# Seven Strassen products for the first four weight blocks of the up projection in eight of eleven steps

## The chip, the core and the metric

One NeuronCore of a Trainium2 chip runs the whole program. The metric is the device time of one execution in microseconds (us), here the median of three runs. Four engines work beside each other, each in the order of its own instruction list, and they hand work over by semaphores: TensorE (PE, with its weight loads PEld), VectorE (DVE), ScalarE (ACT) and GpSimd (POOL). SyncE (SP) issues nearly all DMA transfers.

## The reference, cut to what matters

One transformer block on 256 tokens of width 2048. The change touches the channel mixer's first product alone, `h @ w_up[l]`, which is 256 x 2048 times 2048 x 11264:

```python
h = rmsnorm(x, g_ffn_pre[l])
u = causal_dwconv(h @ w_up[l], ffn_conv_w[l])
gate, val = jnp.split(u, 2, axis=-1)
x = x + rmsnorm((jax.nn.silu(gate) * val) @ w_down[l], g_ffn_post[l])
```

## The kernel before, in words

All weights are float32 and come from device memory once. A block is 256 x 512 weights (512 KB, two slices of 128 rows, `KB = 2`); it lands in one of four buffers `raw` (`RING = 4`). TensorE works on halves of each number: ScalarE rounds a block to `w_hi` (`split` of ScalarE, L608), VectorE subtracts to get `w_lo` (`split` of VectorE, L989), and TensorE adds three matmuls for each pair of operands (activations hi by weights hi, hi by lo, lo by hi; L1486 to L1488). With two slices and two tiles of 128 tokens (`NT = 2`) a block is 12 matmuls of 128 x 512.

The up projection has 11 steps (`NUP`). A step makes 512 gate columns and the 512 value columns that belong to them: 8 blocks into `ACC[0]` (gate, half 0), then 8 into `ACC[1]` (value, half 1), 192 matmuls. Three counters pace the ring. `hi_ready` and `lo_ready` count the blocks that ScalarE and VectorE have split, `block_done` those that TensorE has used. ScalarE may overwrite slot i when `block_done` has reached the block four before; SyncE may load into `raw` slot i once `lo_ready` says that VectorE has read it.

Between the splits the same engines treat the results of the step before, at fixed places in their lists (`gate_done`, `value_done`): ScalarE copies each finished half out of PSUM (`up_evacuate`, L897), SyncE moves its 32 x 32 squares with 16 small transfers (`move_squares`, L482, four after each of four loads), VectorE transposes the squares (`up_turn`, L1316), ScalarE does the first tap of the depthwise convolution (`up_first_tap`, L907), VectorE the other two (`up_tap`, L1323, four instructions each), ScalarE the Silu of the gate (L921), VectorE the product with the value half (L1352), ScalarE rounds it (`act_hi`, L931) and VectorE subtracts (`act_lo`, L1355). Step 0 is written out; steps 1 to 10 are a loop on every engine.

## Time and profile before

| | |
|---|---|
| time, median of 3 runs | 1642.23 us (1642.19 to 1642.34) |
| the profiled execution | 1642.32 us, of which the span of the profile is 1640.5 us |
| PE busy | 1631.4 us (99%) |
| VectorE busy | 1012.3 us (62%) |
| ScalarE busy | 831.9 us (51%) |
| granted TensorE clock over the span | 0.998 |

A busy time is the union of an engine's instructions. Matmuls overlap their neighbours in the trace (0.39 us long, one begun every 0.23 us), so the pace of TensorE is read from what it releases, not from one instruction's length. A row's last bracket says how long the engine was idle before it and who ended that.

### The profile page before, as it was taken

To read this page: it belongs to the slowest core of one execution; us is meant where nothing else is said; L and a number is where in the kernel's file an instruction comes from. 1 tells how busy PE (TensorE), PEld (TensorE's weight loads), DVE (VectorE), ACT (ScalarE), POOL (GpSimd) and SP (SyncE) were. 2 spreads that over 40 slices of the span, in tenths; PEclk is the share of its full clock that TensorE was granted. 3 is DMA by queue.
4 is the path that set the end of the run, shared out by engine and by line. 5 is a ranking of instruction groups with operands and counts; after the bars stand their busy time and mean duration, and the time that the engine had idled before them with its cause. 6 is when DMAs were issued, how large, how long until landed. Compare 5 with 4: busy or idle time off the path is not lost.

```text
span 1640.5 us, 22316 instructions
## 1 busy us (share of the span) xinstructions
PE 1631.4 (99%) x7267; PEld 1346.6 (82%) x7267; DVE 1012.3 (62%) x1374; ACT 831.9 (51%) x1053; POOL 54.6 (3%) x117
## 2 busy tenths in 40 slices
...
GB/s 281 279 225 216 192 181 197 221 214 220 192 206 193 244 215 186 210 226 218 218 221 210 154 219 215 209 220 220 216 215 217 219 224 209 242 192 168 215 197 136
DMA packets 207784, 346.72 MB, mean 211 GB/s; under 512 B 28952, under 2 KB 52329, under 8 KB 207209
## 3 DMA queue, kind: packets, MB, share of 16 engines
...
q0 software_dynamic: 2048, 2.10, 0.4%
...
## 4 chain that ended last, share of the span: by engine, by line
PE 99%; DVE 0%; POOL 0%; DVEq 0%; issue 0%; ACT 0%; POOLq 0%; ACTq 0%
PE PS L1486 29%; PE PS L1488 28%; PE PS L1487 28%; PE PS L1620 3%; PE PS L1618 3%; PE PS L1619 3%; PE PS L1654 1%; PE PS L1656 1%; PE PS L1655 1%; PE PS L1567 0%; PE PS L1578 0%; PE PS L1507 0%; PE PS L1513 0%; PE PS L1501 0%; PE PS L1726 0%; PE PS L1724 0%
## 5 line engine op out<-in xcount | busy, mean ns | idle before, releaser
L989 DVE TENSOR_TENSOR w_lo<-raw,w_hi 128x1024 fp32r<-128x1024 f32 x567 | 690.5, 1224 | 569.4 <-ACT w_hi L608 568.3
L608 ACT ACTIVATE w_hi<-raw 128x1024 fp32r<-128x1024 f32 x567 | 597.5, 1059 | 629.1 <-PE PS L1488 558.7
L1486 PE MATMUL PS<-w_hi,hT_hi 128*128 128x512 f32 x1504 | 587.6, 391 | 0.0
L1488 PE MATMUL PS<-w_hi,hT_lo 128*128 128x512 f32 x1504 | 585.2, 389 | 0.0
L1487 PE MATMUL PS<-w_lo,hT_hi 128*128 128x512 f32 x1504 | 585.1, 389 | 0.0
L1486 PEld LDWEIGHTS PS<-w_hi,hT_hi 128*128 128x128 f32 x1504 | 282.3, 188 | 60.9 <-issue 2.7
L1488 PEld LDWEIGHTS PS<-w_hi,hT_lo 128*128 128x128 f32 x1504 | 282.3, 188 | 58.6
L1487 PEld LDWEIGHTS PS<-w_lo,hT_hi 128*128 128x128 f32 x1504 | 282.3, 188 | 58.5
L1486 PE MATMUL PS<-w_hi,act_hi 128*128 128x512 f32 x336 | 130.9, 390 | 0.0
L1488 PE MATMUL PS<-w_hi,act_lo 128*128 128x512 f32 x336 | 130.7, 389 | 0.0
L1487 PE MATMUL PS<-w_lo,act_hi 128*128 128x512 f32 x336 | 130.7, 389 | 0.0
L1486 PEld LDWEIGHTS PS<-w_hi,act_hi 128*128 128x128 f32 x336 | 63.1, 188 | 13.7 <-issue 0.4
L1487 PEld LDWEIGHTS PS<-w_lo,act_hi 128*128 128x128 f32 x336 | 63.1, 188 | 13.0
L1488 PEld LDWEIGHTS PS<-w_hi,act_lo 128*128 128x128 f32 x336 | 63.1, 188 | 13.0
L1486 PE MATMUL PS<-w_hi,memT_hi 128*128 128x512 f32 x124 | 48.7, 392 | 0.0
L1488 PE MATMUL PS<-w_hi,memT_lo 128*128 128x512 f32 x124 | 48.3, 390 | 0.0
L1487 PE MATMUL PS<-w_lo,memT_hi 128*128 128x512 f32 x124 | 48.2, 389 | 0.0
L897 ACT ACTIVATE up_stage<-PS,r_h 128x512 f32<-128x512 f32 x44 | 27.9, 687 | 36.7 <-PE PS L1488 36.4
L1486 PE MATMUL PS<-w_hi,mixT_hi 128*128 128x512 f32 x96 | 37.3, 389 | 0.0
L1487 PE MATMUL PS<-w_lo,mixT_hi 128*128 128x512 f32 x96 | 37.3, 389 | 0.0
L1488 PE MATMUL PS<-w_hi,mixT_lo 128*128 128x512 f32 x96 | 37.3, 389 | 0.0
L1323 DVE SCALAR_TENSOR_TENSOR value_conv<-turned_sb,up_taps,value_conv 128x255 f32 (+3 forms) x88 | 36.6, 481 | 0.0
...
## 6 DMA issues: line engine op xcount, KB each, us to landing
raw<-in_w_up_dram SPq DMA_DIRECT2D x176, 512.0 KB, 4.0
raw<-in_w_in_dram SPq DMA_DIRECT2D x112, 512.0 KB, 4.1
raw<-in_w_gate_dram SPq DMA_DIRECT2D x96, 512.0 KB, 4.5
raw<-in_w_down_dram SPq DMA_DIRECT2D x88, 512.0 KB, 4.1
raw<-in_w_mem_kv_dram SPq DMA_DIRECT2D x32, 512.0 KB, 5.8
raw<-in_w_o_dram SPq DMA_DIRECT2D x32, 512.0 KB, 4.2
...
raw<-in_w_conv_out_dram SPq DMA_DIRECT2D x16, 512.0 KB, 3.7
```

The lines of the kernel that those rows point to most:

```text
L608: nc.scalar.activation(w_hi[i % RING][:], raw[i % RING][:], ACT.Copy).then_inc(hi_ready, inc)
L897: last = nc.scalar.activation(up_stage[half][:, :, :, t, :], ACC[half][:, t, :].rearrange("p (b m n) -> p m b n", b=BPC, n=SQ), ACT.Copy, ...
L989: nc.vector.tensor_tensor(w_lo[i % RING][:], raw[i % RING][:], w_hi[i % RING][:].bitcast(F32), ALU.subtract).then_inc(lo_ready, inc)
L1323: last = nc.vector.scalar_tensor_tensor(out=d[:, 2 - m:TOK], in0=turned_ch[:, b, 0:TOK - 2 + m], scalar=up_taps[:, m, bass.ds(half * FK + ...
L1486: nc.tensor.matmul(o, a_hi, b_hi, start=first, stop=False)
L1487: nc.tensor.matmul(o, a_hi, b_lo, start=False, stop=False)
L1488: last = nc.tensor.matmul(o, a_lo, b_hi, start=False, stop=last_k)
L1618: nc.tensor.matmul(ACC[1][:, t, :], hi[:, k, s], w_hi[i % RING][:, c, :], start=k == 0, stop=False)
L1619: nc.tensor.matmul(ACC[1][:, t, :], hi[:, k, s], w_lo[i % RING][:, c, :], start=False, stop=False)
L1620: last = nc.tensor.matmul(ACC[1][:, t, :], lo[:, k, s], w_hi[i % RING][:, c, :], start=False, stop=k == HK - 1)
L1654: nc.tensor.matmul(acc[:, t, :], a_hi[:, k, s], b_hi, start=k == 0, stop=False)
L1655: nc.tensor.matmul(acc[:, t, :], a_hi[:, k, s], b_lo, start=False, stop=False)
```

## The change

In steps 1 to 8 the four blocks that cover the first 512 rows of the weights, for gate and value (B11 = rows 0 to 255 of the gate, B12 the same rows of the value, B21 and B22 rows 256 to 511), are multiplied with the four 128 x 256 pieces of the activations by the Winograd form of Strassen's scheme: seven products of 6 matmuls each in place of eight. Sums of activations are made once, in step 0 (`left_sums`). In each fast step VectorE makes four sums of weight blocks (`summed`, the first two in place in `raw`), and the splits of these seven operands take the ring slots. The shared partial results are passed on by ScalarE with four copies out of PSUM (`seed`), two into other PSUM banks, two, scaled, into SBUF (`u2_scaled`, `p5_scaled`). Because these two must be added to the value half, VectorE now copies the value half out (`value_evacuate`, eight instructions) in place of ScalarE. The last two blocks of a fast step are done tile by tile, so that the first value tile is ready 12 matmuls before the end. Steps 9 and 10 do what they did, but are written out.

```diff
+QUAD = 7
+FAST_END = 9
...
+    FASTS = FAST_END - 1
+    STD = 2 * CB - 4
+    FAST_UNITS = -(-(QUAD + STD) // RING) * RING
+    L_DN = N_UP + 2 * NUP * CB
+    N_DN = L_DN + FASTS * (FAST_UNITS - 2 * CB)
...
+u2_scaled = at("u2_scaled", RB + 36 * K, [P, CW])
+p5_scaled = at("p5_scaled", RB + 38 * K, [P, CW])
+S_hi = at("S_hi", RB + 40 * K, [P, 4, KB, P], F32R)
+h2_whole = at("h2_whole", RB + 80 * K, [P, 2 * KB, TOK])
+B_sum = at("B_sum", RB + 80 * K, [P, KB, CW])
+S_sum = at("S_sum", RB + 84 * K, [P, 4, KB, P])
+S_lo = at("S_lo", RB + 84 * K, [P, 4, KB, P], F32R)
...
+    def fast_load(j, m, free, kb, half):
+        sp.wait_ge(lo_ready, up_units(j) + free)
+        if not isinstance(j, int):
+            sp.sem_inc(stream_pace, 1)
+        sp.dma_start(raw[m % RING][:], cols(w_up, kb * KB, half * FF + j * CW)).then_inc(raw_in[m % RING], 16)
+    def fast_step(j, jp):
+        first = isinstance(j, int)
+        for m, (kb, half) in enumerate(((0, 0), (0, 1), (1, 1), (1, 0))):
+            fast_load(j, m, m - 3 if first else (-4, -3, -2, 0)[m], kb, half)
+            move_squares(jp, 0, m)
+        for m in range(4, 2 * CB):
+            half, kb = (0, m - 2) if m < CB + 2 else (1, m - CB)
+            fast_load(j, m, (3, 5, 6, 6)[m - 4] if m < 8 else m, kb, half)
+            if CB <= m < CB + P // SQ:
+                move_squares(jp, 1, m - CB)
     up_step(0, None)
-    up_step(1, 0)
-    with sp.Fori(2, NUP) as j:
+    fast_step(1, 0)
+    with sp.Fori(2, FAST_END) as j:
+        fast_step(j, j - 1)
+    for j in range(FAST_END, NUP):
         up_step(j, j - 1)
...
+        X, Y = ACC[0][:, 1, :], ACC[1][:, 0, :]
+        landed(0)
+        hi(0, raw[0], -3)
+        if not first:
+            landed(3)
+            hi(3, raw[3], -4)
+        summed(1)
+        hi(1, raw[0], -2)
+        if first:
+            up_evacuate(0, 1)
+            landed(3)
+            hi(3, raw[3], 0)
+        summed(3)
+        hi(2, B_sum, -1)
+        seed(ACC[0][:, 0, :], X, 1)
+        hi(0, raw[1], 1)
+        landed(2)
+        hi(1, raw[2], 2)
+        if not first:
+            act.wait_ge(up_out, 2 * jp + 2)
+        seed(u2_scaled[:], X, 3, scale=r_h2[:, 0:1])
+        seed(p5_scaled[:], Y, 2, scale=r_h2[:, 1:2])
+        summed(4)
+        hi(2, B_sum, 3)
+        act.wait_ge(up_out, 2 * jp + 2)
+        seed(ACC[1][:, 1, :], X, 5)
+        for s in range(STD):
+            u = QUAD + s
+            landed(4 + s)
+            hi(u % RING, raw[s % RING], u - RING + 1, 1 if s < STD - 1 else 1 + FAST_UNITS - QUAD - STD)
+            if s in (1, 4):
+                gate_done(jp, {1: 3, 4: 6}[s])
+            if s in (6, 10):
+                value_done(jp, {6: 3, 10: 7}[s])
+            if s == 8:
+                up_evacuate(j, 0)
...
+    def left_sums():
+        a11, a12, a21, a22 = (h2_whole[:, KB * k:KB * k + KB, t * P:(t + 1) * P] for t in range(NT) for k in range(2))
+        dve.wait_ge(block_done, N_UP + CB)
+        dve.wait_ge(mid_lo, len(MID))
+        nc.vector.tensor_tensor(h2_whole[:], h2_hi[:, 0:2 * KB, :].bitcast(F32), h2_lo[:, 0:2 * KB, :].bitcast(F32), ALU.add).then_inc(s_sums, 1)
+        dve.wait_ge(s_sums, 1)
+        nc.vector.tensor_tensor(S_sum[:, 0, :, :], a21, a22, ALU.add).then_inc(s_sums, 1)
+        nc.vector.tensor_tensor(S_sum[:, 2, :, :], a11, a21, ALU.subtract).then_inc(s_sums, 1)
+        dve.wait_ge(s_sums, 2)
+        nc.vector.tensor_tensor(S_sum[:, 1, :, :], S_sum[:, 0, :, :], a11, ALU.subtract).then_inc(s_sums, 1)
+        dve.wait_ge(s_sums, 4)
+        nc.vector.tensor_tensor(S_sum[:, 3, :, :], a12, S_sum[:, 1, :, :], ALU.subtract).then_inc(s_sums, 1)
+    def left_remainders():
+        dve.wait_ge(s_hi_done, 1)
+        nc.vector.tensor_tensor(S_lo[:], S_sum[:], S_hi[:].bitcast(F32), ALU.subtract).then_inc(s_ready, 1)
...
+    def value_evacuate(j, t):
+        if t == 0:
+            dve.wait_ge(value_first, j)
+            dve.wait_ge(up_in[1], 16 * (P // SQ) ** 2 * j)
+        else:
+            dve.wait_ge(block_done, up_units(j) + FAST_UNITS)
+        more = (u2_scaled, p5_scaled)[t]
+        for b in range(BPC):
+            w = slice(b * P, (b + 1) * P)
+            last = nc.vector.scalar_tensor_tensor(out=up_stage[1][:, :, b, t, :], in0=ACC[1][:, t, w].rearrange("p (m n) -> p m n", n=SQ),
+                                                  scalar=r_h2[:, t:t + 1], in1=more[:, w].rearrange("p (m n) -> p m n", n=SQ),
+                                                  op0=ALU.mult, op1=ALU.add)
+        last.then_inc((value_out, up_out)[t], 1)
...
+        def lo(count, slot, src, inc=1):
+            dve.wait_ge(hi_ready, n + count)
+            nc.vector.tensor_tensor(w_lo[slot][:], src[:], w_hi[slot][:].bitcast(F32), ALU.subtract).then_inc(lo_ready, inc)
+        def summed(dst, a, b):
+            nc.vector.tensor_tensor(dst[:], a[:], b[:], ALU.subtract).then_inc(b_sums, 1)
+        b11, b12, b22, b21 = raw
+        lo(1, 0, b11)
+        dve.wait_ge(raw_in[1], up_landed(j, 1))
+        summed(b11, b12, b11)
+        dve.wait_ge(raw_in[2], up_landed(j, 2))
+        summed(b12, b22, b12)
+        dve.wait_ge(b_sums, 4 * jp + 1)
+        summed(B_sum, b22, b11)
+        if not first:
+            lo(2, 3, b21)
+            value_evacuate(jp, 0)
+            lo(3, 1, b11)
+            value_evacuate(jp, 1)
+        else:
+            lo(2, 1, b11)
+            lo(3, 3, b21)
+        lo(4, 2, B_sum)
+        dve.wait_ge(b_sums, 4 * jp + 3)
+        summed(B_sum, b21, B_sum)
+        lo(5, 0, b12)
+        lo(6, 1, b22)
+        lo(7, 2, B_sum)
+        for s in range(STD):
+            u = QUAD + s
+            lo(u + 1, u % RING, raw[s % RING], 1 if s < STD - 1 else 1 + FAST_UNITS - QUAD - STD)
+            if s in (0, 2, 3):
+                gate_done(jp, {0: 2, 2: 4, 3: 5}[s])
+            if s in (5, 7, 8, 9, 11):
+                value_done(jp, {5: 2, 7: 4, 8: 5, 9: 6, 11: 7}[s])
...
+        def product(count, slot, hi, lo, o, start=False):
+            pe.wait_ge(lo_ready, n + count)
+            for c in range(KB):
+                nc.tensor.matmul(o, hi(c), w_hi[slot][:, c, :], start=start and c == 0, stop=False, skip_group_check=not start)
+                nc.tensor.matmul(o, hi(c), w_lo[slot][:, c, :], start=False, stop=False, skip_group_check=not start)
+                last = nc.tensor.matmul(o, lo(c), w_hi[slot][:, c, :], start=False, stop=c == KB - 1, skip_group_check=not start)
+            last.then_inc(block_done, 1)
+        def block(k, t):
+            return [lambda c, a=a: a[:, KB * k + c, t * P:(t + 1) * P] for a in (h2_hi, h2_lo)]
+        def left(m):
+            return [lambda c, a=a: a[:, m, c, :] for a in (S_hi, S_lo)]
+        pe.wait_ge(up_out, 2 * jp + 1)
+        product(1, 0, *block(0, 0), X, True)
+        pe.wait_ge(value_out, jp + 1)
+        product(2 if isinstance(j, int) else 3, 1, *left(0), Y, True)
+        pe.wait_ge(seeded, 4 * jp + 1)
+        product(4, 2, *left(1), X)
+        product(4, 3, *block(1, 0), ACC[0][:, 0, :])
+        pe.wait_ge(seeded, 4 * jp + 2)
+        product(5, 0, *left(2), X)
+        pe.wait_ge(seeded, 4 * jp + 3)
+        product(6, 1, *left(3), Y)
+        pe.wait_ge(seeded, 4 * jp + 4)
+        product(7, 2, *block(1, 1), X)
+        for u in range(QUAD, QUAD + CB - 2):
+            multiply(n, u, CB, h2_hi, h2_lo, lambda t: ACC[0][:, t, :], kb=2 + u - QUAD, onto=True)
+        for u in range(QUAD + CB - 2, QUAD + STD - 2):
+            multiply(n, u, CB, h2_hi, h2_lo, lambda t: ACC[1][:, t, :], kb=4 + u - QUAD - CB, onto=True)
+        for t in range(NT):
+            for u in range(QUAD + STD - 2, QUAD + STD):
+                if t == 0:
+                    pe.wait_ge(lo_ready, n + u + 1)
+                for c in range(KB):
+                    k, sl = DK + KB * (u - QUAD - STD) + c, slice(t * P, (t + 1) * P)
+                    b_hi, b_lo = w_hi[u % RING][:, c, :], w_lo[u % RING][:, c, :]
+                    nc.tensor.matmul(ACC[1][:, t, :], h2_hi[:, k, sl], b_hi, start=False, stop=False, skip_group_check=True)
+                    nc.tensor.matmul(ACC[1][:, t, :], h2_hi[:, k, sl], b_lo, start=False, stop=False, skip_group_check=True)
+                    last = nc.tensor.matmul(ACC[1][:, t, :], h2_lo[:, k, sl], b_hi, start=False, stop=k == DK - 1, skip_group_check=True)
...
```

VectorE, at the head of the loop over the steps. `w_lo_57` to `w_lo_60` are the four ring slots, `raw_49` to `raw_52` the four landing buffers. Before:

```order
L989 TENSOR_TENSOR w_lo_57<-raw_49,w_hi_53 128x1024 [waits hi_ready]
L988 REGISTER_ALU
L989 TENSOR_TENSOR w_lo_58<-raw_50,w_hi_54 128x1024 [waits hi_ready]
L988 REGISTER_ALU
L989 TENSOR_TENSOR w_lo_59<-raw_51,w_hi_55 128x1024 [waits hi_ready]
L1312 REGISTER_ALU
L1314 ISA [waits up_in_gate]
```

After (the row ahead of these is the split of `raw_49`, as before):

```order
L1589 TENSOR_TENSOR raw_49<-raw_50,raw_49 128x1024 [waits raw_in1]
L1589 TENSOR_TENSOR raw_50<-raw_51,raw_50 128x1024 [waits raw_in2]
L1597 ISA
L1589 TENSOR_TENSOR B_sum<-raw_51,raw_49 128x1024 [waits b_sums]
L1585 REGISTER_ALU
L1586 TENSOR_TENSOR w_lo_60<-raw_52,w_hi_56 128x1024 [waits hi_ready]
L1569 REGISTER_ALU [waits value_first]
L1575 SCALAR_TENSOR_TENSOR up_stage_168<-PS,r_h_76,u_scaled 128x4x32 [waits up_in_value]
L1575 SCALAR_TENSOR_TENSOR up_stage_168<-PS,r_h_76,u_scaled 128x4x32 x3
L1585 REGISTER_ALU
L1586 TENSOR_TENSOR w_lo_58<-raw_49,w_hi_54 128x1024 [waits hi_ready]
L1571 ISA
```

Three weight sums and the first half of the value copy now stand between the step's first split and its third.

ScalarE, at the same place. Before:

```order
L607 REGISTER_ALU [waits raw_in0]
L608 ACT_TABLE_LOAD
L608 ACTIVATE w_hi_53<-raw_49 128x1024 [waits block_done]
L607 REGISTER_ALU [waits raw_in1]
L608 ACTIVATE w_hi_54<-raw_50 128x1024 [waits block_done]
L607 REGISTER_ALU [waits raw_in2]
L608 ACTIVATE w_hi_55<-raw_51 128x1024 [waits block_done]
```

After:

```order
L1004 ISA [waits raw_in0]
L1005 ACTIVATE w_hi_53<-raw_49 128x1024 [waits block_done]
L1004 REGISTER_ALU [waits raw_in3]
L1005 ACTIVATE w_hi_56<-raw_52 128x1024 [waits block_done]
L1011 ISA
L1004 REGISTER_ALU [waits b_sums]
L1005 ACTIVATE w_hi_54<-raw_49 128x1024 [waits block_done]
L1011 REGISTER_ALU
L1004 REGISTER_ALU [waits b_sums]
L1005 ACTIVATE w_hi_55<-B_sum 128x1024 [waits block_done]
```

The second split is now that of `raw_52`, the fourth load, and the activation table is no longer loaded at the head of the loop.

ScalarE, at the Silu of the gate within the loop. Before:

```order
L607 REGISTER_ALU [waits raw_in2]
L608 ACTIVATE w_hi_55<-raw_51 128x1024 [waits block_done]
L921 ACT_TABLE_LOAD [waits up_conv]
L921 ACTIVATE gate_conv<-gate_conv 128x1024
L607 REGISTER_ALU [waits raw_in3]
```

After:

```order
L1004 REGISTER_ALU [waits raw_in0]
L1005 ACTIVATE w_hi_56<-raw_49 128x1024 [waits block_done]
L969 ACTIVATE gate_conv<-gate_conv 128x1024 [waits up_conv]
L1004 REGISTER_ALU [waits raw_in1]
L1005 ACTIVATE w_hi_53<-raw_50 128x1024 [waits block_done]
```

The table load ahead of the Silu is gone from the loop as well; one stands in step 1, ahead of it.

## Rows read from the trace of the kernel before

**Rows 1.** Page, part 1: span, and busy time of each engine

```profile
span 1640.5 us, 22316 instructions
...
PE 1631.4 (99%) x7267; PEld 1346.6 (82%) x7267; DVE 1012.3 (62%) x1374; ACT 831.9 (51%) x1053; POOL 54.6 (3%) x117
```

**Rows 2.** Page, part 4: shares of the chain that ended last, by engine

```profile
PE 99%; DVE 0%; POOL 0%; DVEq 0%; issue 0%; ACT 0%; POOLq 0%; ACTq 0%
```

**Rows 3.** Windows: one up step, and the time after the last matmul

```profile
core 0: us, PE busy (x) PEld busy (x) DVE busy (x) ACT busy (x) POOL busy (x), PEclk, DMA share, GB/s
...
980.03:1023.56 43.53, 43.53 (x194) 36.05 (x193) 30.34 (x43) 26.73 (x33) 0.00 (x0) 1.00 0.71 213
...
1632.90:1640.50 7.60, 0.03 (x1) 0.00 (x0) 3.50 (x6) 0.69 (x2) 0.73 (x2) 0.67 0.50 188
```

**Rows 4.** Waits from 900 to 1380 us: total us, times, longest us

```profile
DVE w_lo L989 <- ACT w_hi L608: 140.6, 97, 2.3
ACT w_hi L608 <- PE PS L1488: 116.5, 85, 1.7
```

**Rows 5.** Timeline of ACT: start us, length us, instruction, count, idle before and releaser

```profile
980.03 1.27 ACT L897 ACTIVATE up_stage<-PS,r_h 128x512 f32<-128x512 f32 x2 [1.74 <-PE PS L1488]
981.18 1.06 ACT L608 ACTIVATE w_hi<-raw 128x1024 fp32r<-128x1024 f32 x1
982.13 1.70 ACT L907 ACTIVATE value_conv<-turned_sb,up_taps 128x256 f32 x4
983.73 1.05 ACT L608 ACTIVATE w_hi<-raw 128x1024 fp32r<-128x1024 f32 x1
...
992.72 1.06 ACT L931 ACTIVATE act_hi<-value_conv  x1 [0.83 <-DVE value_conv L1352]
...
998.98 1.06 ACT L608 ACTIVATE w_hi<-raw 128x1024 fp32r<-128x1024 f32 x1 [1.65 <-PE PS L1488]
...
1012.20 1.28 ACT L921 ACT_TABLE_LOAD   x1 [1.28 <-DVE gate_conv L1323]
1013.50 1.06 ACT L921 ACTIVATE gate_conv<-gate_conv  x1
1014.46 1.99 ACT L608 ACTIVATE w_hi<-raw 128x1024 fp32r<-128x1024 f32 x2
```

**Rows 6.** Timeline of DVE in the same step

```profile
985.96 1.66 DVE L1323 SCALAR_TENSOR_TENSOR value_conv<-turned_sb,up_taps,value_conv 128x255 f32 x4
987.54 1.22 DVE L989 TENSOR_TENSOR w_lo<-raw,w_hi 128x1024 fp32r<-128x1024 f32 x1
...
991.39 1.21 DVE L1352 TENSOR_TENSOR value_conv<-gate_conv,value_conv  x1
...
1000.08 1.23 DVE L989 TENSOR_TENSOR w_lo<-raw,w_hi 128x1024 fp32r<-128x1024 f32 x1 [1.49 <-ACT w_hi L608]
1001.22 1.42 DVE L1316 STREAM_TRANSPOSE turned_sb<-up_moved 128x256 f32<-128x256 f32 x4
...
1010.44 1.66 DVE L1323 SCALAR_TENSOR_TENSOR gate_conv<-turned_sb,up_taps,gate_conv 128x254 f32 x4
```

**Rows 7.** Timeline of DVE at an evacuation of PSUM with two operands

```profile
190.09 2.15 DVE L1047 SCALAR_TENSOR_TENSOR proj_stage<-PS,r_x,cc_sb 128x128 f32<-128x128 f32 x8
192.25 0.69 DVE L1124 TENSOR_REDUCE top<-PS 128x2 f32<-128x512 f32 x1
```

**Rows 8.** Timeline of the SP queue, issues in the same step

```profile
989.80 0.39 SPq L325 DMA_DIRECT2D raw<-in_w_up_dram  x1
990.23 2.41 SPq L482 DMA_DIRECT2D up_moved<-up_stage  x4
992.97 0.38 SPq L325 DMA_DIRECT2D raw<-in_w_up_dram  x1
```

**Rows 9.** DMA issues of the up weights: count, KB each, median us to landing

```profile
raw<-in_w_up_dram SPq DMA_DIRECT2D x176, 512.0 KB, 4.0
```

**Rows 10.** Timeline of PE, its last matmul

```profile
1632.54 0.39 PE L1726 MATMUL PS<-w_hi,act_lo 128*128 128x512 f32 x1
```

More of the change, by code:

```diff
@@ L277, in build_block_kernel @@
         mix_sq, mix_sum, x_new, h2_sq = (sem(n) for n in ("mix_sq", "mix_sum", "x_new", "h2_sq"))
+        s_sums, s_hi_done, s_ready, b_sums, seeded = (sem(n) for n in ("s_sums", "s_hi_done", "s_ready", "b_sums", "seeded"))
+        value_first, value_out = sem("value_first"), sem("value_out")
         silu_done, prod_done, act_hi_done, act_lo_done = (sem(n) for n in ("silu_done", "prod_done", "act_hi_done", "act_lo_done"))
@@ L305, in value_block, with up_units, up_landed @@
             return value_conv[:, bass.ds(BPC * j + b, 1), :].rearrange("p a t -> p (a t)")
+        def up_units(j):
+            if not isinstance(j, int) or 0 < j <= FAST_END:
+                return N_UP + 2 * CB - FAST_UNITS + FAST_UNITS * j
+            return N_UP + 2 * CB * j + (FASTS * (FAST_UNITS - 2 * CB) if j else 0)
+        def up_landed(j, m):
+            return 4 * N_UP + 8 * CB * j + 16 * (m // RING + 1)
         def down_landed(j, i):
             per_chunk = len(range(i % RING, DB, RING))
-            return 4 * N_DN + 16 * (j * per_chunk + i // RING + 1)
+            return 4 * L_DN + 16 * (j * per_chunk + i // RING + 1)
         @block.sync
@@ L889, in up_evacuate @@
             def up_evacuate(j, half):
-                act.wait_ge(block_done, N_UP + CB * (2 * j + half + 1))
+                fast = not isinstance(j, int) or 1 <= j < FAST_END
+                act.wait_ge(block_done, up_units(j) + (QUAD + CB - 2 if fast else CB * (half + 1)))
                 if isinstance(j, int) and j == 0:
@@ L898, in up_evacuate @@
                                                 ACT.Copy, scale=r_h2[:, t:t + 1])
+                    if half and t == 0:
+                        last.then_inc(value_out, 1)
                 last.then_inc(up_out, 1)
@@ L911, in gate_done @@
             def gate_done(j, i):
-                if i == 2:
+                if i == 2 and not 1 <= j < FAST_END:
                     up_evacuate(j, 1)
@@ L933, in up_step @@
             def up_step(j, jp):
-                n = N_UP + 2 * CB * j
+                n = up_units(j)
                 if jp is None:
@@ L938, in up_step @@
                     for i in range(CB):
-                        split(n, i)
+                        split(n, i, up_landed(j, i))
                         gate_done(jp, i)
                 for i in range(CB):
-                    split(n, CB + i)
+                    split(n, CB + i, up_landed(j, CB + i))
                     if jp is not None:
@@ L946, in up_step, with fast_step, hi, landed @@
                         up_evacuate(j, 0)
+                    if jp is None and i == 6:
+                        act.wait_ge(s_sums, 5)
+                        nc.scalar.activation(S_hi[:], S_sum[:], ACT.Copy).then_inc(s_hi_done, 1)
+            def fast_step(j, jp):
+                n = up_units(j)
+                first = isinstance(j, int)
+                def hi(slot, src, free, inc=1):
+                    act.wait_ge(block_done, n + free)
+                    nc.scalar.activation(w_hi[slot][:], src[:], ACT.Copy).then_inc(hi_ready, inc)
+                def landed(m):
+                    act.wait_ge(raw_in[m % RING], up_landed(j, m))
+                def summed(k):
+                    act.wait_ge(b_sums, 4 * jp + k)
+                def seed(dst, src, done, **scale):
+                    act.wait_ge(block_done, n + done)
+                    nc.scalar.activation(dst, src, ACT.Copy, **scale).then_inc(seeded, 1)
+                X, Y = ACC[0][:, 1, :], ACC[1][:, 0, :]
[34 more added lines that the diff above has]
+                        up_evacuate(j, 0)
@@ L948, in _ @@
             up_step(0, None)
-            with act.Fori(1, NUP) as j:
+            fast_step(1, 0)
+            with act.Fori(2, FAST_END) as j:
+                fast_step(j, j - 1)
+            for j in range(FAST_END, NUP):
                 up_step(j, j - 1)
@@ L1424, in up_step @@
                         split(n, i)
+                        if jp == FAST_END - 1 and i < NT:
+                            value_evacuate(jp, i)
                         gate_done(jp, i)
@@ new lines, in fast_step @@
+            def fast_step(j, jp):
+                n = up_units(j)
+                first = isinstance(j, int)
+                def lo(count, slot, src, inc=1):
[32 more added lines that the diff above has]
+                        value_done(jp, {5: 2, 7: 4, 8: 5, 9: 6, 11: 7}[s])
@@ L1431, in _ @@
             up_step(0, None)
-            with dve.Fori(1, NUP) as j:
+            fast_step(1, 0)
+            with dve.Fori(2, FAST_END) as j:
+                fast_step(j, j - 1)
+            for j in range(FAST_END, NUP):
                 up_step(j, j - 1)
@@ L1485, in multiply @@
                         a_hi, a_lo, b_hi, b_lo = hi[:, k, s], lo[:, k, s], w_hi[i % RING][:, c, :], w_lo[i % RING][:, c, :]
-                        nc.tensor.matmul(o, a_hi, b_hi, start=first, stop=False)
-                        nc.tensor.matmul(o, a_hi, b_lo, start=False, stop=False)
-                        last = nc.tensor.matmul(o, a_lo, b_hi, start=False, stop=last_k)
+                        nc.tensor.matmul(o, a_hi, b_hi, start=first, stop=False, skip_group_check=onto)
+                        nc.tensor.matmul(o, a_hi, b_lo, start=False, stop=False, skip_group_check=onto)
+                        last = nc.tensor.matmul(o, a_lo, b_hi, start=False, stop=last_k, skip_group_check=onto)
                 last.then_inc(block_done, inc)
```

23 lines of the change are left out of this document (17 added, 6 removed).

## Prediction

> **What bounds the kernel now.** I read the page's busy times first: TensorE is busy 1631.4 of 1640.5 us, VectorE 62%, ScalarE 51% [rows 1]. The chain that ended last says the same: 99% of it is TensorE [rows 2]. So the window over one up step is 43.53 us long with TensorE busy in all of it [rows 3]; the code has 192 matmuls there, 0.2267 us each, and a block of 12 takes 2.72 us. Removing matmuls pays only as long as the other engines keep up, so the waits come next: each split on VectorE waits for ScalarE's and ScalarE's for TensorE [rows 4]. The helpers run up to four blocks ahead and are held back by the ring, never the reverse. The timelines of ScalarE and VectorE [rows 5, 6] then give each helper's duration and the time until the next instruction may start. The question is whether the new list still fits a shorter step.
>
> **What is saved.** One product of 6 matmuls in each of 8 steps: 48 x 0.2267 = 10.9 us. A fast step needs 186 matmuls, 42.16 us, 1.36 less than before. Two table loads a step leave ScalarE's loop too (the order shows it), 1.28 us each [rows 5].
>
> **What is added, per fast step.** VectorE: three more splits, four weight sums, and the value copy that ScalarE did. A split is followed by the next instruction after 1.14 us (it is 1.22 long) [rows 6]. The trace has no sum of two raw blocks. The nearest row is the product of gate and value, float32 of the same size with both inputs in SBUF, 1.21 long [rows 6]; the split costs as much. I take 1.14; the bounds are 0.6 (two elements per cycle) and 1.3. The value copy has its like in the projection phase: eight instructions, PSUM and SBUF in, strided out, 2.16 us from the first to the next other instruction, so 1.07 for a tile [rows 7]. ScalarE: three more splits (1.06 long, next after 0.95) and four copies of 512 columns; two such copies with what follows take 1.15, so 0.58 each [rows 5]. A copy from PSUM into PSUM isn't in the trace; between 0.5 and 1.1, I take 0.58, since only the length differs from a known row. VectorE's list then holds 19 splits, 4 sums, 4 x 1.58 of taps [rows 6], 2.7 of transposes, 2 more full-size instructions and 2.1 of copying: 39.6 us of the 42.2. Nothing is left for waits, and the waits are in the order.
>
> **The walk round one step.** I followed the loop's order on each engine with these durations, a hand-over costing 0.04 us (ScalarE's split starts at 998.98, ends at 1000.04, VectorE starts at 1000.08) or, where the waiting engine first computes addresses, 0.10 (taps end at 1012.10, ScalarE starts at 1012.20) [rows 5, 6]. For the start of ScalarE's taps I take 0.19 (bounds 0.04 and 0.3), and for TensorE's restart after a wait 0.24: one weight load of 0.19 plus a hand-over, where the whole 0 to 0.4 is open. The products are p1 to p7, the twelve plain blocks s0 to s11. It closes on itself like this, from the start of p3:
> 1. p3 and p4, 2.72; p5 until its last matmul ends, 5 x 0.2267 + 0.39 = 1.52; 0.04. Sum 4.28.
> 2. ScalarE's fourth copy 0.58, its split of s0's weights 1.06, 0.04: VectorE's split of s0 starts at 5.96.
> 3. That split 1.14, the gate's transposes 1.42, hand-over 0.19, ScalarE's four taps 1.60, its split of s2's weights 1.10: 11.41. The taps stand ahead of that split in ScalarE's list, so what is queued behind their wait is the ring.
> 4. Split 1.14, taps 1.58, split 1.14, taps until their end 1.66, 0.10, Silu 0.96, ScalarE's split of s5's weights 1.10: 19.09.
> 5. The same as 3 for the value half: 24.54.
> 6. Split 1.14, taps 1.58, split 1.22 (s8): this frees the first landing buffer. Now SyncE has to issue the next step's four loads with the gate's moves after each. One load with four moves takes 3.17 us (989.80 to 992.97) [rows 8]. Its fourth load, B21, therefore goes out three such rounds later, 9.51, and lands 3.9 after (median 4.0 [rows 9], 3.6 to 4.4). ScalarE splits B21 second, ahead of the next two: 1.10. With 0.04 that is 18.49, so 43.03.
> 7. VectorE: split of B21 1.14, value copy 1.07, split of B12-B11 1.14, value copy 1.07, split of the third operand 1.22, restart 0.24: 5.88. Sum **48.9 us**, and p3 of the next step begins.
>
> So the helpers' loop takes 48.9 us where TensorE needs 42.2. TensorE idles 6.7 us a step: about 5.2 ahead of p2 (waiting for the split of B12-B11), 0.8 ahead of p3 (its operand comes 2.2 after p2's, and p2 takes 1.36), 0.6 ahead of s0. The sums are hidden beside B21's landing: at 1.14 each they are done 1.5 us before its split, so even half that price changes nothing there.
>
> **The sum.** Seven steps (2 to 8) at 48.9 - 43.5 = 5.4: 37.8. Step 1 has other waits (its blocks come from a plain step, ScalarE copies the value half): the same walk gives TensorE 2.3 idle ahead of p3, and 0.6, 0.8 and 0.5 at s0, s5 and s11, 4.3 less 1.36, so +2.9. Steps 9 and 10 are back at 43.53. The activation sums of step 0 are two full-size and four quarter-size instructions, some 3.6 us on VectorE with a ring of four blocks (10.9 us) in hand: nothing. Together +40.7.
>
> **The clock.** The gap ahead of p2 is new in kind. The only idle stretch of TensorE in the trace is the end: the last matmul ends at 1632.93 [rows 10], and of the 7.60 us after it 0.67 of full clock was granted [rows 3]. With half clock as the other level, that is full for about 2.6 us, then half. Five us of waiting is longer. If the clock falls in the gap and is back soon after, p2 costs 6 x 0.2267 = 1.36 more, of which 0.8 hides in the wait ahead of p3: 0.55 a step, 7 steps, 3.9. I take this in: +44.6. Against the profiled execution: span 1640.5 + 44.6 = 1685.1, and the 1.8 around it give 1686.9; the median of before, 1642.23, lies 0.1 under the profiled 1642.32, so **1687**. The Trainium skill (TensorE: Matmul & The Clock Gate, "HAM oscillation") says that a burst after a long enough wait for data starts at half clock, and does so in every round of such a loop. The trace of before has no such round to show it; by the page the loop would be at the upper of my two figures and not at +40.7.
>
> **Rivals.**
> - *The clock stays down longer*, from p2 to p5: 24 matmuls dearer by 0.2267, less 0.8, 4.6 a step on the loop; with seven steps 32 in place of 3.9. Up to 1715; anywhere between 1697 and there. For it: p2 and p3 are short bursts with a gap between. Against: from p3 on TensorE works without a break. 12%.
> - *Only the step's edge costs.* If B21 is there in time (shorter moves or landings) and the helpers regain their lead, what is left is the chain from the end of s9 (5.44 before p1): the last matmul's end 0.16 after its slot, split on ScalarE with its two hand-overs, then on VectorE split, three sums, split, copy, split, and the restart: 0.16 + 1.14 + 1.14 + 3.42 + 1.14 + 1.07 + 1.22 + 0.24, so p2 starts at 4.1 in place of 1.36: 2.7. With 0.8 and 0.6 that is 4.1 a step against 1.36 saved: +2.8, eight times, 22: 1665. This is a floor that I can't get round, since all of it is in VectorE's order; with the sums at 0.6 it is 1651. 16%.
> - *Faster: TensorE stays the bound* and the 10.9 us come through: 1631. Its one condition is the loop of the helpers at 42.2 or less, with the operands of p2 and p3 ready on time; break-even is at 43.5, 5.4 us shorter than I count. It would take VectorE to do all sums and the copy beside other work, or instructions in row that overlap far more than the rows show. For it: TensorE was 99% busy and VectorE has 13 us free per step. Against: those 13 us are all used up. 4%.
> - *The gain and the waits cancel*, within 0.2%: 2%.
>
> **How the numbers follow.** The forecast has 62%, its own range 1677 to 1697: hand-overs at their low ends take 6 off, a landing at 3.6 takes 2, no clock loss 4; their upper ends add as much. 4% are left for beyond 1715. The range 1668 to 1705 takes in half of each neighbour. A change of 0.2%, 3.3 us, is about what a measurement of this kernel can tell from none. Slower by more has 94%, within it 2%, faster 4%.
>
> **What would show it.** In the profile after: up steps of about 49 us for steps 2 to 8 and 43.5 for 9 and 10; TensorE's longest idle ahead of the matmuls on `S_hi` and `S_lo` (p2), released by VectorE's `w_lo`; PE busy near 96%, spans of VectorE without a gap around the step's edge; B21's load issued about 3 us apart from the one before and ScalarE waiting for it; the granted clock a little under full. Sums clearly under 1.1 us, or value copies under 0.8, would be the first error; a B21 that waits for nothing the second. An up step of 42.2 would refute the whole walk.

## The result, and the profile after

The changed kernel takes 1708.2 us (median of 4 runs, 1707.4 to 1708.6) against 1642.2 before: 66.0 us slower, ratio 1.0401 with a 95% interval of 1.0383 to 1.0419. The forecast was 1687, its range 1668 to 1705: the direction was right, the time lies above the range.

The page of the changed kernel: span, busy times, the granted clock in 40 slices, and the chain that ended last by engine and by line.

```profile
span 1706.2 us, 22099 instructions
...
PE 1648.2 (97%) x7219; PEld 1344.5 (79%) x7219; DVE 1094.3 (64%) x1500; ACT 834.0 (49%) x1075; POOL 54.2 (3%) x117
...
PEclk9999999999999999999999999999999999999999
...
PE 78%; SPq 8%; DVE 4%; DMA 4%; issue 3%; ACT 2%; DVEq 0%; ACTq 0%; POOL 0%; POOLq 0%
PE PS L1679 21%; PE PS L1680 21%; PE PS L1681 21%; SPq L507 7%; DMA raw<-in_w_up_dram 3%; PE PS L1811 3%; PE PS L1813 3%; PE PS L1812 3%; DVE w_lo L1586 2%; ACT w_hi L1005 2%; SPq L522 1%; PE PS L1895 1%; PE PS L1896 1%; PE PS L1897 1%; DVE
```

TensorE is idle in the span for 58 us, where it was for 9 [rows 1]. Its share of the last chain has gone from 99% to 78% [rows 2], and what took the place is not one engine: SyncE's issues (L507 are the square moves), a load's landing, VectorE, ScalarE. A chain that passes through so many hands reads like a loop of hand-overs in which no engine is full; the experiments test that. A slice of the clock's row is 43 us long, so a few us at half clock don't show in it.

Windows: one fast step from p2 to p2, then three pieces around the p2 at its end, then steps 9 and 10.

```profile
core 0: us, PE busy (x) PEld busy (x) DVE busy (x) ACT busy (x) POOL busy (x), PEclk, DMA share, GB/s
1116.68:1169.69 53.01, 46.72 (x186) 36.52 (x186) 40.19 (x58) 27.36 (x35) 0.00 (x0) 0.92 0.60 178
1163.00:1167.00 4.00, 1.14 (x6) 0.60 (x4) 1.93 (x3) 1.85 (x2) 0.00 (x0) 1.00 0.40 141
1167.40:1173.90 6.50, 4.21 (x10) 3.35 (x11) 6.50 (x13) 3.22 (x4) 0.00 (x0) 0.50 0.27 81
1174.10:1200.00 25.90, 25.16 (x109) 19.98 (x108) 17.01 (x26) 15.50 (x22) 0.00 (x0) 1.00 0.69 211
1371.80:1415.32 43.52, 43.52 (x194) 36.04 (x192) 33.33 (x48) 23.62 (x29) 0.00 (x0) 1.00 0.78 239
1415.32:1458.84 43.52, 43.52 (x194) 36.03 (x192) 30.84 (x44) 24.14 (x30) 0.00 (x0) 1.00 0.73 224
```

This fast step is 53.0 us long, TensorE busy in 46.7 of it, VectorE in 40.2. From one p3 to the next, which is called a round from here on, the seven rounds of the run take 51.35 to 53.02 us, 52.3 in the mean. The plain steps at the end take 43.5 as before [rows 3]. The third row shows a clock at half; in the gap ahead of p2 it was still full up to 1167 (second row).

Waits of TensorE over the whole run (total us, times, longest us):

```profile
PE PS L1895 <- DVE w_lo L1586: 41.0, 8, 5.7
```

Seven of these eight waits (L1895, `product`) stand ahead of p2, 5.37 to 5.75 us each; the eighth, 2.07 us, is ahead of step 1's p3. Timeline of TensorE at one of them: the end of p1, p2, the start of p3, and the start of p3 one round later.

```profile
1163.75 0.39 PE L1897 MATMUL PS<-w_hi,hT_lo 128*128 128x512 f32 x1
1169.69 0.80 PE L1895 MATMUL PS<-w_hi,S_hi 128*128 128x512 f32 x1 [5.55 <-DVE w_lo L1586]
1170.29 0.63 PE L1896 MATMUL PS<-w_lo,S_hi 128*128 128x512 f32 x1
1170.71 0.63 PE L1897 MATMUL PS<-w_hi,S_lo 128*128 128x512 f32 x1
...
1172.42 0.63 PE L1895 MATMUL PS<-w_hi,S_hi 128*128 128x512 f32 x1
...
1224.84 0.58 PE L1895 MATMUL PS<-w_hi,S_hi 128*128 128x512 f32 x1
```

p2 begins 5.55 us after the last matmul of p1 has ended, when VectorE has made the split of B12-B11. Matmuls then begin 0.43 us apart in place of 0.23: TensorE runs at half clock (1.2 GHz) after the wait, until 1174. The page of the Trainium skill that the prediction named (TensorE: Matmul & The Clock Gate, "HAM oscillation") has a loop of short bursts and waits in which each burst starts at half clock. This trace agrees: seven waits of 5.37 to 5.75 us, and behind each of them 0.43 us a matmul.

Timeline of VectorE through the edge of the same step and, below the dots, at the value half's transposes:

```profile
1160.54 2.50 DVE L1589 TENSOR_TENSOR raw<-raw,raw 128x1024 f32<-128x1024 f32 x2
1162.95 1.22 DVE L1589 TENSOR_TENSOR B_sum<-raw,raw 128x1024 f32<-128x1024 f32 x1
1166.24 1.23 DVE L1586 TENSOR_TENSOR w_lo<-raw,w_hi 128x1024 fp32r<-128x1024 f32 x1 [2.07 <-ACT w_hi L1005]
1167.38 1.12 DVE L1575 SCALAR_TENSOR_TENSOR up_stage<-PS,r_h,u_scaled 128x128 f32<-128x128 f32 x4
1168.42 1.22 DVE L1586 TENSOR_TENSOR w_lo<-raw,w_hi 128x1024 fp32r<-128x1024 f32 x1
...
1171.72 1.22 DVE L1589 TENSOR_TENSOR B_sum<-raw,B_sum 128x1024 f32<-128x1024 f32 x1
1172.85 2.35 DVE L1586 TENSOR_TENSOR w_lo<-raw,w_hi 128x1024 fp32r<-128x1024 f32 x2
...
1179.09 1.23 DVE L1586 TENSOR_TENSOR w_lo<-raw,w_hi 128x1024 fp32r<-128x1024 f32 x1 [0.86 <-ACT w_hi L1005]
...
1184.59 1.23 DVE L1586 TENSOR_TENSOR w_lo<-raw,w_hi 128x1024 fp32r<-128x1024 f32 x1 [1.83 <-ACT w_hi L1005]
...
1192.27 1.22 DVE L1586 TENSOR_TENSOR w_lo<-raw,w_hi 128x1024 fp32r<-128x1024 f32 x1 [1.02 <-ACT w_hi L1005]
1195.07 1.42 DVE L1425 STREAM_TRANSPOSE turned_sb<-up_moved 128x256 f32<-128x256 f32 x4 [1.58 <-DMA up_moved<-up_stage]
...
1199.40 1.23 DVE L1586 TENSOR_TENSOR w_lo<-raw,w_hi 128x1024 fp32r<-128x1024 f32 x1 [1.80 <-ACT w_hi L1005]
...
1218.66 1.23 DVE L1586 TENSOR_TENSOR w_lo<-raw,w_hi 128x1024 fp32r<-128x1024 f32 x1 [2.00 <-ACT w_hi L1005]
```

Timeline of SyncE's queue for the same step (the last five rows from a narrower window, which shows single issues):

```profile
1157.94 0.38 SPq L522 DMA_DIRECT2D raw<-in_w_up_dram  x1
1158.36 2.40 SPq L507 DMA_DIRECT2D up_moved<-up_stage  x4
1161.10 0.38 SPq L522 DMA_DIRECT2D raw<-in_w_up_dram  x1
...
1181.18 2.42 SPq L507 DMA_DIRECT2D up_moved<-up_stage  x4
...
1190.65 2.40 SPq L507 DMA_DIRECT2D up_moved<-up_stage  x4
...
1203.57 0.38 SPq L522 DMA_DIRECT2D raw<-in_w_up_dram  x1
1204.31 2.43 SPq L507 DMA_DIRECT2D up_moved<-up_stage  x4
1207.09 0.38 SPq L522 DMA_DIRECT2D raw<-in_w_up_dram  x1
...
1210.25 0.38 SPq L522 DMA_DIRECT2D raw<-in_w_up_dram  x1
...
1213.40 0.38 SPq L522 DMA_DIRECT2D raw<-in_w_up_dram  x1
```

The queue goes in groups of one load and four moves, 3.16 us each, the first group of a step 3.5. B21's load goes out at 1161.10, behind three such groups; VectorE's split of it starts at 1166.24, after a wait of 2.07. The value half's moves go out from 1181.18 to 1193.05, and VectorE, which had waited 1.58 us for them to land, begins its transposes at 1195.07.

Timeline of ScalarE in the same step: the copy of p5's result from PSUM to PSUM, and the split that waits for B21's load (B21 is the first of the two splits merged in the row).

```profile
1177.51 0.58 ACT L1015 ACTIVATE PS<-PS 128x512 f32<-128x512 f32 x1 [0.54 <-PE PS L1897]
...
1217.57 2.00 ACT L1005 ACTIVATE w_hi<-raw 128x1024 fp32r<-128x1024 f32 x2 [7.28 <-DMA raw<-in_w_up_dram]
```

### The profile page after: what moved, and what is told of

It is laid out like the page before. It is cut to its first block, busy times and chain, and to the rows that moved or that the text cites. A ratio compares the mean times of both kernels' runs of the same rounds, so it can differ in the third digit from the quotient of the medians.

```text
span 1706.2 us, 22099 instructions
## 1 busy us (share of the span) xinstructions
PE 1648.2 (97%) x7219; PEld 1344.5 (79%) x7219; DVE 1094.3 (64%) x1500; ACT 834.0 (49%) x1075; POOL 54.2 (3%) x117
## 4 chain that ended last, share of the span: by engine, by line
PE 78%; SPq 8%; DVE 4%; DMA 4%; issue 3%; ACT 2%; DVEq 0%; ACTq 0%; POOL 0%; POOLq 0%
PE PS L1679 21%; PE PS L1680 21%; PE PS L1681 21%; SPq L507 7%; DMA raw<-in_w_up_dram 3%; PE PS L1811 3%; PE PS L1813 3%; PE PS L1812 3%; DVE w_lo L1586 2%; ACT w_hi L1005 2%; SPq L522 1%; PE PS L1895 1%; PE PS L1896 1%; PE PS L1897 1%; DVE value_conv L1432 1%
## 5 line engine op out<-in xcount | busy, mean ns | idle before, releaser
L1098 DVE TENSOR_TENSOR w_lo<-raw,w_hi 128x1024 fp32r<-128x1024 f32 x439 | 534.8, 1224 | 451.5 <-ACT w_hi L653 450.3
L1679 PE MATMUL PS<-w_hi,hT_hi 128*128 128x512 f32 x1312 | 516.8, 394 | 6.5 <-DVE w_lo L1586 6.4
L1680 PE MATMUL PS<-w_lo,hT_hi 128*128 128x512 f32 x1312 | 511.5, 390 | 0.0
L1681 PE MATMUL PS<-w_hi,hT_lo 128*128 128x512 f32 x1312 | 511.5, 390 | 0.0
L1679 PEld LDWEIGHTS PS<-w_hi,hT_hi 128*128 128x128 f32 x1312 | 246.3, 188 | 72.2 <-DVE w_lo L1586 16.7
L1681 PEld LDWEIGHTS PS<-w_hi,hT_lo 128*128 128x128 f32 x1312 | 246.4, 188 | 52.2
L1680 PEld LDWEIGHTS PS<-w_lo,hT_hi 128*128 128x128 f32 x1312 | 246.5, 188 | 48.6
L1586 DVE TENSOR_TENSOR w_lo<-raw,w_hi 128x1024 fp32r<-128x1024 f32 x136 | 164.9, 1218 | 70.0 <-ACT w_hi L1005 70.0
L1895 PE MATMUL PS<-w_hi,S_hi 128*128 128x512 f32 x64 | 32.1, 501 | 41.0 <-DVE w_lo L1586 41.0
L1895 PEld LDWEIGHTS PS<-w_hi,S_hi 128*128 128x128 f32 x64 | 15.4, 241 | 47.7 <-DVE w_lo L1586 41.9
L1425 DVE STREAM_TRANSPOSE turned_sb<-up_moved 128x256 f32<-128x256 f32 x88 | 31.3, 412 | 18.3 <-DMA up_moved<-up_stage 18.3
```

Of the source, the lines that this page charges most:

```text
L1098: nc.vector.tensor_tensor(w_lo[i % RING][:], raw[i % RING][:], w_hi[i % RING][:].bitcast(F32), ALU.subtract).then_inc(lo_ready, inc)
L1586: nc.vector.tensor_tensor(w_lo[slot][:], src[:], w_hi[slot][:].bitcast(F32), ALU.subtract).then_inc(lo_ready, inc)
L1679: nc.tensor.matmul(o, a_hi, b_hi, start=first, stop=False, skip_group_check=onto)
L1680: nc.tensor.matmul(o, a_hi, b_lo, start=False, stop=False, skip_group_check=onto)
L1681: last = nc.tensor.matmul(o, a_lo, b_hi, start=False, stop=last_k, skip_group_check=onto)
L1895: nc.tensor.matmul(o, hi(c), w_hi[slot][:, c, :], start=start and c == 0, stop=False, skip_group_check=not start)
```

## The experiments

Each is compared with the kernel before on the same chip, which took 1642.1 to 1642.3 us beside them. "After" is the changed kernel, 1708.2. The steps of the walk are those of the table in the next section.

**e1_warm: the clock alone.** Spare matmuls fill the wait ahead of p2.

```diff
+if not isinstance(j, int):
+    for _ in range(22):
+        nc.tensor.matmul(PS[:, 4, 0:P], ident[:], ident[:], start=True, stop=True)
 pe.wait_ge(value_out, jp + 1)
```

Expected: 

> The changed kernel (1708.2 us) with 22 spare matmuls of 128 x 128 into an unused PSUM bank between p1 and p2 in steps 2 to 8, 4.7 us of work in a gap of 5.8, so that TensorE is not idle there. It tells what the fallen clock costs. Theory A (the walk round the helpers' loop sets the time, and the clock adds to it only where p2 to p5 stand in the loop): the clock stays at full, p2 and p3 end 1.1 us a step earlier, 7 steps, 1708 - 8 = 1700 (1697 to 1703); the gap ahead of p2 stays 5.4 to 5.8 wide as measured from the end of p1's matmuls to p2. Theory B (the clock is the main cause of the loss): well under 1680.

Measured: 1704.1 us (ratio 1.0375, 1.0358 to 1.0392), 4.1 less than after. A step of it:

```profile
1118.60:1170.65 52.05, 49.06 (x231) 39.33 (x232) 40.19 (x59) 27.64 (x35) 0.00 (x0) 1.00 0.61 181
```

The clock stays at full, and the step is still 52.1 us long. Theory B has fallen. Theory A had the sign and twice the size, and 1704.1 lies above its range. VectorE's rows show where the rest went. After, and below the dots e1, at the value half's transposes of the same step:

```profile
1142.77 1.42 DVE L1425 STREAM_TRANSPOSE turned_sb<-up_moved 128x256 f32<-128x256 f32 x4 [1.48 <-DMA up_moved<-up_stage]
...
1143.62 1.42 DVE L1425 STREAM_TRANSPOSE turned_sb<-up_moved 128x256 f32<-128x256 f32 x4 [2.58 <-DMA up_moved<-up_stage]
```

Over the last six rounds the walk's steps 1 and 7, where p2 and p3 stand, give back 7.8 us, 1.3 a round; but VectorE waits longer for the value half's moves, above all in three of the rounds (2.52 to 2.84 us), and the walk's step 5 takes 3.5 us of that away. The first round is 1.0 us longer than after's: its p3 to p5, where no spare matmuls stand, ran at a granted clock of 0.72 in this execution, and at 1.00 in after's. So the fallen clock is dearer than the 4 us that e1 wins, though far from the 66. Why the moves landed later in three rounds stays open.

**e2_nosums: the weight sums left out in steps 2 to 8.**

```diff
-nc.vector.tensor_tensor(dst[:], a[:], b[:], ALU.subtract).then_inc(b_sums, 1)
+if first:
+    nc.vector.tensor_tensor(dst[:], a[:], b[:], ALU.subtract).then_inc(b_sums, 1)
+else:
+    dve.sem_inc(b_sums, 1)
```

Expected: 

> The four weight sums are left out in steps 2 to 8, the operands being whatever the buffers hold; splits, products and all waits stay. VectorE has 4.6 us less in each of seven steps. Theory A (the sums lie beside the landing of B21 and the fourth behind p3 is off the loop): 1705 to 1709. Theory C (the amount of VectorE's work sets the time): 1708 - 32 = 1676.

Measured: 1708.7 us (1.0404, 1.0386 to 1.0421): nothing gained from 4 x 7 instructions less on the engine that ends nearly every wait of TensorE. VectorE at the step's edge:

```profile
1166.87 1.23 DVE L1586 TENSOR_TENSOR w_lo<-raw,w_hi 128x1024 fp32r<-128x1024 f32 x1 [5.64 <-ACT w_hi L1005]
```

Its wait for B21's split is now 5.64 in place of 2.07: the sums' time has turned into waiting. Theory C has fallen for this kernel.

**e3_order: the third and fourth load ahead of the last two groups of moves.**

```diff
 for m, (kb, half) in enumerate(((0, 0), (0, 1), (1, 1), (1, 0))):
     fast_load(j, m, m - 3 if first else (-4, -3, -2, 0)[m], kb, half)
-    move_squares(jp, 0, m)
+    if m < 2:
+        move_squares(jp, 0, m)
+move_squares(jp, 0, 2)
+move_squares(jp, 0, 3)
```

Expected: 

> SyncE issues loads three and four (B22, B21) ahead of the last two of the four groups of square moves, at the head of each fast step; nothing else differs. B21 can go out when VectorE has read the slot, some 2.8 us sooner. Theory A: the split of B21 on VectorE starts about 2 us sooner, as it then waits for the third sum instead, 7 steps: 1708 - 14 = 1694 (1690 to 1698). Theory C (VectorE's amount) and theory B (clock) leave it at 1706 to 1709.

Measured: 1699.0 us (1.0351, 1.0334 to 1.0369), 9.2 less. No work was taken away, only the order in a queue of transfers. VectorE at the edge:

```profile
1157.89 1.23 DVE L1589 TENSOR_TENSOR w_lo<-raw,w_hi 128x1024 fp32r<-128x1024 f32 x1 [0.28 <-ACT w_hi L1008]
```

The wait ahead of B21's split is 0.28 now. The sign and the mechanism are as theory A had them; of the 14 us expected 9 came, and 1699.0 lies 1 us above its range.

**e4_lean: TensorE's work cut by 87 us.** The third matmul of each three is left out of the plain blocks of steps 1 to 8 (in the last two blocks, which are done tile by tile, by the same edit).

```diff
-nc.tensor.matmul(o, a_hi, b_lo, start=False, stop=False, skip_group_check=onto)
-last = nc.tensor.matmul(o, a_lo, b_hi, start=False, stop=last_k, skip_group_check=onto)
+last = nc.tensor.matmul(o, a_hi, b_lo, start=False, stop=onto and last_k, skip_group_check=onto)
+if not onto:
+    last = nc.tensor.matmul(o, a_lo, b_hi, start=False, stop=last_k, skip_group_check=onto)
```

Expected: 

> In steps 1 to 8 the third of each three matmuls (activations lo by weights hi) is left out of the twelve plain blocks: 48 matmuls or 10.9 us of TensorE less a step, 87 us in all. Theory A (TensorE's count is off the loop but for p3 to p5): 1700 to 1712. Theory D (TensorE is still the bound and the waits come on top of its work): about 1708 - 87 = 1621.

Measured: 1708.3 us (1.0401, 1.0384 to 1.0419). A step of it:

```profile
1119.13:1170.99 51.86, 38.39 (x139) 27.43 (x139) 40.18 (x58) 27.27 (x35) 0.00 (x0) 0.89 0.63 182
```

TensorE is busy in 38.4 of 51.9 us, 8 less than after. Its rounds take 51.81 to 53.91 us, so they are no shorter. Theory D has fallen: the amount of TensorE's work in the plain blocks doesn't bound a fast step. What is on the walked loop is its run from p3 to p5, and e4 leaves that as it is. That the 1.36 us which Strassen saves a step can't show either is argued from this; no run tests it.

**e5_moves: e3, and the value half's moves two loads earlier.**

```diff
-if CB <= m < CB + P // SQ:
-    move_squares(jp, 1, m - CB)
+if CB - 2 <= m < CB - 2 + P // SQ:
+    move_squares(jp, 1, m - CB + 2)
```

Expected: 

> e3_order (1699.0 us) and, in addition, the value half's square moves stand two loads earlier in SyncE's list (behind the 7th to 10th load of a fast step in place of the 9th to 12th). In e3 VectorE waits 1.64 us a step for these squares at the value half's transposes, and that wait is on the walked loop. Theory A: the wait goes, 7 steps by about 1.4: 1689 (1685 to 1692). If the loop did not run through SyncE's moves (theory C, VectorE's amount of work): 1697 to 1700.

Measured: 1682.1 us (1.0241, 1.0224 to 1.0258), 16.9 less than e3, more than the 10 expected and below theory A's range. The walk's step 5 takes 5.28 to 5.48 us in e5's rounds, where it took 7.06 to 7.80 in e3's: 13.1 us over the seven. An eighth wait of this kind, 1.58 us in step 8, is gone too; what the last 2 us are was not taken apart. VectorE at the value half's transposes, which begin now without a wait:

```profile
1177.73 1.22 DVE L1589 TENSOR_TENSOR w_lo<-raw,w_hi 128x1024 fp32r<-128x1024 f32 x1 [1.02 <-ACT w_hi L1008]
1178.88 1.42 DVE L1428 STREAM_TRANSPOSE turned_sb<-up_moved 128x256 f32<-128x256 f32 x4
```

**e6_stagger: e5, and ScalarE's and VectorE's follow-up work one block later.**

```diff
-if s in (1, 4):
-    gate_done(jp, {1: 3, 4: 6}[s])
-if s in (6, 10):
-    value_done(jp, {6: 3, 10: 7}[s])
+if s in (2, 5):
+    gate_done(jp, {2: 3, 5: 6}[s])
+if s in (7, 11):
+    value_done(jp, {7: 3, 11: 7}[s])
...
-if s in (0, 2, 3):
-    gate_done(jp, {0: 2, 2: 4, 3: 5}[s])
-if s in (5, 7, 8, 9, 11):
-    value_done(jp, {5: 2, 7: 4, 8: 5, 9: 6, 11: 7}[s])
+if s in (0, 3, 4):
+    gate_done(jp, {0: 2, 3: 4, 4: 5}[s])
+if s in (5, 8, 9, 10, 11):
+    value_done(jp, {5: 2, 8: 4, 9: 5, 10: 6, 11: 7}[s])
```

Expected: 

> e5_moves and, in addition, ScalarE's first taps, Silu and the rounding of the product, with VectorE's taps and product that follow them, stand one block later in their engines' lists in the fast steps, so that a split is not queued behind a wait for the engine that has just begun the work ahead. No work is added or left out. Theory A: the hand-overs to and fro leave the loop in part, 1.3 us a step: about 10 less than e5_moves, 1679 (1674 to 1684). Theory C (VectorE's amount): no change from e5_moves.

Measured: 1669.0 us (1.0165, 1.0148 to 1.0182), 13.1 less than e5 where about 10 had been expected (and below the range, as e5 already was). Three changes of order, with all the work in place, have taken back 39 of the 66 us. A step of it:

```profile
1100.70:1147.64 46.94, 43.05 (x186) 34.68 (x186) 40.29 (x58) 28.09 (x35) 0.00 (x0) 0.99 0.66 201
```

TensorE is busy in 43.1 of 46.9 us, VectorE in 40.3.

**e8_floor: e6 with the sums of steps 2 to 8 left out** (the edit of e2 on e6).

Expected: 

> e6_stagger with the four weight sums left out in steps 2 to 8 (the operands are whatever the buffers hold). In e2_nosums, where other links set the loop, leaving them out gave nothing. Theory A: with these links shortened the sums at the step's edge and VectorE's amount come into the loop, so it now gives 7 x 1.6 = 11 us less than e6_stagger, 1668 (1662 to 1676). If something else still sets the loop: as e6_stagger.

Measured: 1660.5 us (1.0111, 1.0094 to 1.0128), 8.5 less than e6; the saving is near the 11 expected, and the time lies below the range because e6 did. The same edit that gave nothing in e2 counts here, with the links beside it shorter. Even without the sums the kernel is 18 us behind the one before.

**e7_peeled: the kernel before with steps 1, 9 and 10 written out**, so that the table loads leave ScalarE's loop (the same edit on every engine).

```diff
-with act.Fori(1, NUP) as j:
+up_step(1, 0)
+with act.Fori(2, 9) as j:
+    up_step(j, j - 1)
+for j in range(9, NUP):
     up_step(j, j - 1)
```

Expected: 

> The kernel before with steps 1, 9 and 10 written out as in the change and no Strassen step: the two activation table loads per step go from ScalarE's loop, TensorE's work stays. With TensorE the bound throughout, theory A gives no change: 1642.2, within 0.5. If the table loads or the loops' ends cost anything: up to 20 us less (2 x 1.29 x 8).

Measured: 1642.3 us (1.0000, 0.9990 to 1.0009). ScalarE's busy time falls from 831.9 [rows 1] to 807.9 us, the time does not move: this side effect of the change is worth nothing where TensorE is the bound.

**e9_actcopy: the value half copied out by ScalarE again**, its two added terms left out.

```diff
 hi(1, raw[0], -2)
+if not first:
+    act.wait_ge(block_done, n)
+    act.wait_ge(up_in[1], 16 * (P // SQ) ** 2 * jp)
+    for t in range(NT):
+        last = nc.scalar.activation(up_stage[1][:, :, :, t, :], ACC[1][:, t, :].rearrange("p (b m n) -> p m b n", b=BPC, n=SQ),
+                                    ACT.Copy, scale=r_h2[:, t:t + 1])
+        last.then_inc((value_out, up_out)[t], 1)
...
-    value_evacuate(jp, 0)
     lo(3, 1, b11)
-    value_evacuate(jp, 1)
```

Expected: 

> The changed kernel with the value half copied out by ScalarE again in steps 2 to 8 (two copies behind its third split of the step), so that VectorE has 2.1 us less at the step's edge. The two terms that VectorE adds in this copy are left out. Theory A: p2 waits for one split less one copy, and p3 for ScalarE's split, which now stands behind the copies: 1.3 us a step sooner, 1708 - 9 = 1699 (1694 to 1703). Theory C (VectorE's amount sets the time): 1708 - 15 = 1693, as far as the loop follows it in full. If the copy is beside the loop: 1708.

Measured: 1700.1 us (1.0356, 1.0339 to 1.0373), 8.1 less: the copy stands on the loop, and moving it gives what the walk says, not the 15 us of its length. The walk's step 7 takes 5.14 us in the first three rounds, and at most that in the others, where it took 6.18.

**e10_half: four fast steps in place of eight** (`FAST_END = 5`).

Expected: 

> The changed kernel with four fast steps (1 to 4) in place of eight. A fast step in the loop took 52.4 us against 43.5, step 1 some 4 more than a plain one. Theory A (the cost is one per step and nothing lies outside the steps): 1642.2 + 4 + 3 x 8.9 = 1673 (1670 to 1676). If part of the cost is paid once (sums of activations, longer program, its fetching): above, up to 1690.

Measured: 1673.8 us (1.0192, 1.0175 to 1.0209), as theory A had it. The cost is paid per step: four fast steps less are 34.4 us less, 8.6 each.

## Why the prediction was wrong

The mechanism, slower by the helpers' loop and not by TensorE, was right, and the runs bear it out: taking 87 us of matmuls away gives nothing (e4), taking 28 VectorE instructions away gives nothing (e2), and reordering alone gives 39 us (e3, e5, e6). The sum was 21 us short. Its steps, for the round whose rows are shown above (from the start of one p3 at 1172.42 to the next at 1224.84; steps' ends are the starts of ScalarE's fourth copy, 1177.51, and of VectorE's splits at 1179.09, 1184.59, 1192.27, 1199.40 and 1218.66), and for all seven rounds, read in the same way:

| step of the walk | forecast us | this round | mean of seven (lowest to highest) |
|---|---|---|---|
| 1, p3 to p5 | 4.28 | 5.09 | 5.06 (4.39 to 5.93) |
| 2, to the split of s0 | 1.68 | 1.58 | 1.58 (1.57 to 1.58) |
| 3, to the split of s2 | 5.45 | 5.50 | 5.47 (5.29 to 5.50) |
| 4, to the split of s5 | 7.68 | 7.68 | 7.67 (7.59 to 7.68) |
| 5, to the split of s7 | 5.45 | 7.13 | 7.23 (6.93 to 7.82) |
| 6, to the split of B21 | 18.49 | 19.26 | 19.15 (19.00 to 19.34) |
| 7, to p3 | 5.88 | 6.18 | 6.18 (6.17 to 6.18) |
| sum | 48.9 | 52.4 | 52.3 (51.35 to 53.02) |

The step that failed is **"The same as 3 for the value half"**. It isn't the same: the gate half's squares are moved at the head of the step, long before VectorE transposes them, but the value half's four groups of moves stand behind the ninth load, which waits for VectorE's split of s0. They go out from 1181.18 to 1193.05, and VectorE waits 1.58 us for their landing, until 1195.07. I had walked each engine's list and had taken the moves' landing as long past. So this step was 1.8 us a round too short, 12.5 of the 21 us. e5 shows that the wait is on the loop: with the moves two loads earlier it is gone, the step takes 5.28 to 5.48 us, and the kernel 17 us less.

Two terms were mis-sized. **The clock**: I counted it behind p2 alone, 0.55 a step. It stays down into p3, in some rounds longer than in others, so the first row of the table varies from 4.39 to 5.93. The first and the last row together are 1.1 over the walk without the clock, and e1, with the clock full, has them 1.3 shorter than after in the six rounds named there: twice what I took, or more. That e1 as a whole won 4.1 us, next to the 3.9 of the forecast, is chance, since longer waits for the moves and the dearer first round took back half of it. **B21's load**: SyncE issued the first load 0.22 us after VectorE's split of s8 had ended, where I had nothing; the three groups of load and moves took 9.83 in place of 9.51 (1203.57 to 1213.40), as the first is 3.52 long; and ScalarE's split of B21 began 4.17 after the issue where I had 3.9 for the landing. Over the seven rounds this step of the walk was 0.66 too short each, 4.6 us in all.

Together: 12.5 us for the walk's step 5, 4.6 for 6, and 3.7 for 1 and 7 beyond the 3.9 that had been taken in for the clock, less 0.6 in the others: 20 of the 21 us. The rest, about 1 us, lies outside the seven rounds. Smaller slips of the prediction changed little: the four waits of the kernel's step 1 add up to 4.2 and not 4.3; TensorE's restart is 0.05 us and not 0.24 (the split of B12-B11, begun at 1168.42 and 1.22 long, ends 0.05 before p2); and in the trace of before TensorE has another idle stretch beside the end, 1.6 us at the start of the run.

What was right: seven rounds of one kind and steps 9 and 10 at 43.5; some 4 us for all that lies outside the seven rounds (66.0 less seven times 8.8; forecast 2.9); the longest idle ahead of p2, 5.55 for 5.2; a sum at 1.13 (from 1171.72 to the next start) and a copied tile at 1.04; the sums hidden beside B21's landing; the table loads worth nothing. My floor for the order at the step's edge, 1665 with the other links shortened, was met nearly by e6, 1669. The 1651 that I gave for sums at 0.6 us was too low: e8, with no sums at all, has 1660.5. None of the runs beat the kernel before: with the sums left out and the order mended it is still 18 us away. What those 18 are made of was not taken apart.
